# ScalarE splits three weight units of the first expert instead of four ahead of the routing, and loads its function table between the second and the third

## The reference, cut to what matters

```
h = h + rglru_mixer(h, ...)                   # ends with an output projection
logits = rms_norm(h, g) @ router_w            # 256 x 8
top_vals, top_idx = lax.top_k(logits, 2)
top_w = softmax(top_vals)
gates = sum(one_hot(top_idx) * top_w)
for e in range(8):
    y = y + gates[:, e] * ((silu(x @ w_gate[e]) * (x @ w_up[e])) @ w_down[e])
h = h + y
```

## Time and profile before

| what | value |
|---|---|
| median of 3 executions | 1358.57 us (1357.74 to 1360.34) |
| profiled execution, its own time | 1354.03 us |
| profiled execution, its span | 1352.2 us |
| TensorE busy | 1316.0 us (97%) |
| VectorE busy | 799.3 us (59%) |
| ScalarE busy | 639.1 us (47%) |
| mean granted TensorE clock | 0.991 |

### The profile page before, as it was taken

How to read it: one execution, slowest core, us unless ns; L and a number is a source line. 1 busy time by engine, 2 the same in 40 slices (tenths; PEclk the granted TensorE clock), 3 DMA queues, 4 the chain that set the end, 5 groups by cost and what they waited for, 6 DMA issues and landing times.

```text
span 1352.2 us, 18615 instructions
## 1 busy us (share of the span) xinstructions
PE 1316.0 (97%) x7440; PEld 995.3 (74%) x7440; DVE 799.3 (59%) x832; ACT 639.1 (47%) x591; POOL 0.4 (0%) x6
## 2 busy tenths in 40 slices
PE   8999999999999899999999999999999999999997
PEld 7988999999999788884357885346887345888432
DVE  7995565655599679971039981009983105987100
ACT  5486534443488567741048760008872005875000
POOL 0000000000000000000000000000000000000000
PEclk9999999999999979999999999999999999999999
DMA  9332555455365599999999999999999999999996
GB/s 333 128 94 63 156 166 178 138 193 178 111 196 194 223 363 362 363 366 346 406 413 411 409 411 403 401 407 410 414 409 408 412 409 410 412 406 413 409 408 271
DMA packets 149893, 426.13 MB, mean 315 GB/s; under 512 B 7728, under 2 KB 65712, under 8 KB 135472
## 3 DMA queue, kind: packets, MB, share of 16 engines
q1 hardware_dynamic: 149808, 424.90, 82.7%
HBM read 423.82 MB, written 1.05 MB: 314 GB/s over the span
## 4 chain that ended last, share of the span: by engine, by line
PE 77%; DMA 8%; DVE 7%; ACT 3%; issue 3%; SPq 2%; DVEq 0%; ACTq 0%
PE P L1688 55%; PE P L2125 12%; DMA over_gates_raw<-in_moe_w_gate 6%; PE P L2149 3%; DVE cacc L1115 2%; DVE raw_lo L1075 2%; DMA over_xb_raw<-in_moe_w_down 2%; PE P L2012 1%; SPq L602 1%; PE P L2033 1%; DMA raw<-in_w_in_even 1%; PE P L2067 1%; ACT whi L929 1%; PE P L1721 1%; PE P L2030 1%
## 5 line engine op out<-in xcount | busy, mean ns | idle before, releaser
L1443 DVE TENSOR_TENSOR raw_lo<-raw,whi 128x2048 fp32r<-128x2048 f32 x84 | 189.3, 2288 | 10.8 <-ACT whi L929 10.2
L1688 PE MATMUL P<-hn_hi,whi 128*128 128x272 f32 (+1 forms) x640 | 186.4, 291 | 0.5 <-ACT ig L867 0.2
L929 ACT ACTIVATE whi<-raw 128x2048 fp32r<-128x2048 f32 x84 | 161.1, 1920 | 54.2 <-PE P L1688 32.9
L1688 PE MATMUL P<-whi,xe_hi 128*128 128x512 f32 x448 | 179.1, 400 | 7.1 <-DVE over_gates_lo L1443 7.1
L1688 PE MATMUL P<-hn_hi,raw_lo 128*128 128x272 f32 (+1 forms) x640 | 184.5, 288 | 0.0
L1688 PE MATMUL P<-hn_lo,whi 128*128 128x272 f32 (+1 forms) x640 | 183.8, 287 | 0.0
L1688 PE MATMUL P<-whi,xe_lo 128*128 128x512 f32 x448 | 177.3, 396 | 0.0
L1443 DVE TENSOR_TENSOR over_gates_lo<-over_gates_raw,whi 128x2048 fp32r<-128x2048 f32 x72 | 162.9, 2289 | 19.2 <-ACT whi L929 19.1
L1075 DVE TENSOR_TENSOR raw_lo<-raw,whi 128x2048 fp32r<-128x2048 f32 (+4 forms) x71 | 148.1, 2105 | 41.6 <-ACT whi L662 41.5
L929 ACT ACTIVATE whi<-over_gates_raw 128x2048 fp32r<-128x2048 f32 x72 | 137.6, 1919 | 43.1 <-PE P L1688 17.9
L1663 DVE TENSOR_TENSOR hb<-silu,P 128x512 f32<-128x512 f32 (+1 forms) x16 | 9.9, 621 | 220.2 <-PE P L2125 220.2
(11 more groups left out here) (298 smaller groups left out, 2054.4 us busy)
## 6 DMA issues: line engine op xcount, KB each, us to landing
raw<-in_moe_w_up SPq DMA_DIRECT2D x64, 1024.0 KB, 15.3
raw<-in_moe_w_gate SPq DMA_DIRECT2D x64, 1024.0 KB, 15.1
over_gates_raw<-in_moe_w_down SPq DMA_DIRECT2D x64, 1024.0 KB, 16.3
over_gates_raw<-in_moe_w_gate SPq DMA_DIRECT2D x48, 1024.0 KB, 18.5
raw<-in_moe_w_down SPq DMA_DIRECT2D x40, 1024.0 KB, 15.6
over_gates_raw<-in_moe_w_up SPq DMA_DIRECT2D x32, 1024.0 KB, 16.4
over_xb_raw<-in_moe_w_up SPq DMA_DIRECT2D x16, 1024.0 KB, 15.0
raw<-in_ffn_w_gate SPq DMA_DIRECT2D x10, 1024.0 KB, 5.3
```

Of the source, the lines that this page charges most:

```text
L929: act.activation(whi[u % HI][:, :], moe_raw[k % MOE_RAW][:, :], ACT.Copy).then_inc(hi_ready, 1)
L1443: dve.tensor_tensor(moe_lo(k), moe_raw[k % MOE_RAW][:, :], whi[u % HI][:, :].bitcast(F32), ALU.subtract).then_inc(lo_ready, 1)
L1688: last = pe.matmul(dst, lhs, rhs, start=start and n == 0, stop=stop and n == 2)
```

## The change

ScalarE's list changes, and no other engine's. The split of unit 3 moves from ahead of the routing's steps to behind them, and the load of the table with the square root moves from behind unit 3 to between units 1 and 2.

```diff
-            for k in range(4):
+            for k in range(3):
+                if k == 2:
+                    act.preload_act_table_set("sqrt_and_others")
                 split_item_hi(0, k)
...
-            act.preload_act_table_set("sqrt_and_others")
             def squares(c):
...
             act.activation(st[:, 6:8], st[:, 4:6], ACT.Sqrt).then_inc(h2_root, 1)
-            for k in range(4, READY):
+            for k in range(3, READY):
                 split_item_hi(0, k)
```

## The result

| | before | after |
|---|---|---|
| median of 17 executions each | 1360.16 us (1357.51 to 1363.3) | 1353.26 us (1348.31 to 1357.16) |
| ratio after / before | | 0.9963, 95% interval 0.9951 to 0.9976 |
| span of the profiled execution | 1352.2 us | 1350.0 us |

By the measured ratio the change makes the kernel faster by 0.37%, 5.0 us of 1358.57; the interval reaches from 3.3 to 6.7 us. The two medians lie 6.9 us apart, which is more than that, so only the size of some 5 us is sure and not its tenths. The forecast was 1353.5 us.

What follows compares the result with a forecast made beforehand. The routing was taken to wait for unit 3's transfer through its split in ScalarE's list. Terms 2.78 + 2.3 + 0 = 5.1 us took the median from 1358.57 to 1353.5 us, range 1350.8 to 1356.8.

Steps and rivals of the forecast that it cites:

- What bounds: Ahead of the router's product: routing waits for unit 3's weight transfer, because its split stands ahead in ScalarE's list.
- Table load moved, at no cost: ScalarE, between units 1 and 2: the 1.28 us load delays nothing, with 1.66 us to spare before the residual's half 0.
- First term: Routing up to the router's product: squares and copy come earlier, so the product starts at 470.27 instead of 473.05, 2.78 us.
- Second term: Router's product on TensorE: all 32 matmuls end before the clock falls, 3.6 us instead of 5.91, gaining 2.3 us.
- the idle stretch: TensorE's 2.99 us of idle time ahead of the router's product; with it gone, the clock's fall should not come earlier.
- Third term: Gather on TensorE, 5.82 us before: gain taken as 0, with -0.9 and +2.1 us as bounds.
- Three splits in a row: ScalarE behind the root: three splits take 5.55 us, just use up the 4.26 us idle time and cost nothing.
- Does it last to the end?: Expert 0 to the end: transfers catch up within expert 0, then fixed data at fixed rate, so the end moves 5.1 us.

Runs made afterwards that it cites:

- units only: Kernel before with only unit 3's split moved behind the root, the table load left where it was, now behind unit 2; ratio to before 0.9949.
- three loads: Changed kernel with two more table loads, of other sets, ahead of the one between units 1 and 2; ratio to before 0.9979.
- the filled one: Kernel before with 20 more matmuls, results unused, where TensorE was idle ahead of the router's product; ratio to before 0.9994.
- two ahead: Changed kernel with two units instead of three split ahead of the routing, four in a row behind the root; ratio to before 0.9956.
- before again: Kernel before, unaltered, timed against itself for a second trace; ratio 1.0002.
- before with the attention filled: Kernel before with 8 more matmuls, results unused, in the first layer's attention, where TensorE waits at 96 to 97 us; ratio to before 0.9997.

## Why the prediction was right

*What bounds.* Right. The units only kernel shows that unit 3's split, waiting for its transfer, was what the routing waited for.

*Table load moved, at no cost.* Right: 1.28 us, unit 2's split from 464.67, 1.47 us to spare (1.66 forecast). It also brought nothing, since with three units the load fits behind unit 2 as well. The three loads kernel confirms the price and the point from which it hurts.

*First term, 2.78 us.* Measured 6.49 - 3.70 = 2.79 us.

*Second term, 2.3 us.* In the first pair of traces 5.89 - 3.71 = 2.18 us. On average of the traces it is larger: the three traces of before with nothing added to the routing have 5.89, 6.59 and 6.97 us, the five of the kernels whose product starts at +3.70 and with nothing added there all have 3.71, which makes 6.48 - 3.71 = 2.8 us. What I wrote about its cause was half right. The fall did not come earlier, but it comes without the idle stretch too: the filled one did not stop it, and in three loads it came 5.5 us behind the residual with only 1.01 us of idle time ahead of the product. In 13 traces it came 5.5 to 8.7 us behind the residual. The product that ends at +7.4 is ahead of ten of these falls, the one that starts at +6.5 met the fall in all four of its traces. A fall at +5.5 would catch the changed kernel too. In the seven traces whose product starts at +3.70 or +3.34 it came at +7.7 to +8.7; whether the earlier product keeps early falls away or these seven had luck is not shown.

The timed executions fit the split into two terms. Each has a mean granted clock on record. Among executions with the same clock, those of the changed kernel, units only and two ahead (47 in all) are on average 2.6 us quicker than the 102 of before, near the first term's 2.78 (one execution of before, at 1873 us, is left out). The rest of their advantage, 1.3 of 3.9 us, goes with a higher mean clock, 0.9900 against 0.9887.

*Third term, 0.* The gather took 5.42 us instead of 5.82 in the first pair, 6.73 in the second trace of the changed kernel and 6.75 in the second of before, a little above the 6.7 that I took as the worst. Its length goes up and down with the clock's return, on both sides.

*Three splits in a row.* Right; 0.29 us of idle time was left. That cover is gone with a fourth (two ahead), and it still costs nothing.

*Does it last to the end?* Up to the end of expert 0, wholly. The windows of the changed kernel that answer to the earlier trace rows:

```profile
490.00:492.50 2.50, 2.50 (x12) 2.03 (x11) 2.50 (x2) 1.92 (x1) 0.00 (x0) 1.00 1.02 401
...
600.00:613.70 13.70, 13.70 (x77) 8.92 (x77) 0.69 (x1) 1.64 (x3) 0.00 (x0) 1.00 0.76 260
640.00:700.00 60.00, 56.54 (x307) 25.40 (x304) 9.55 (x9) 10.73 (x11) 0.00 (x0) 1.00 1.03 410
```

The gap at 490 us is filled, and expert 0's output is copied at 608.58 us instead of 613.74, 5.16 us earlier. But the span shrank by 2.2 us only. The stretch from that copy to the end took 738.5 us before and 741.4 after. I had said that behind expert 0 there is a fixed amount of data at a fixed rate; that is the step of the prediction that did not hold. The same sum was right for the median and too large by 2.9 us for this pair of traces, so that 5.0 us came out so near to 5.1 is in part luck; the second timing of the changed kernel gave 0.9982, 2.4 us. From copy to copy of the large experts' outputs and the small ones', the changed kernel's trace loses 1.6 us between 913.75 and 1039.24 (125.5 us, against 123.9 from 919.00 to 1042.94) and 1.9 us behind it until 1132.61 (93.4 against 91.4); what differs elsewhere, +0.7, -0.7 and -0.4 us, comes to about nothing. At the head of the first of these stretches, where the fourth expert after expert 0, a large one, begins, the windows of the changed kernel show the clock (all engines):

```profile
912.00:916.00 4.00, 4.00 (x12) 3.10 (x11) 3.73 (x2) 3.84 (x3) 0.00 (x0) 0.57 1.03 410
```

It was low for 3.4 us from 912.4 on. TensorE loses half of that in an expert in which it is hardly quicker than the transfers. That it then frees slots later than they are wanted at that expert's end is my reading. The windows of 1000 to 1100 us, before, then after:

```profile
1000.00:1100.00 100.00, 97.84 (x454) 54.22 (x454) 29.95 (x25) 23.27 (x20) 0.00 (x0) 1.00 1.02 412
```

```profile
1000.00:1100.00 100.00, 97.84 (x448) 52.35 (x448) 26.45 (x23) 20.49 (x18) 0.00 (x0) 0.98 1.00 394
```

The other traces show the price of such a fall in its own stretch. There are three stretches from a small expert's copy to the next large one's in each of the 13 traces. In 22 of these 39 the clock fell shortly ahead of the small expert's copy (at 701 to 705, 912 to 921, or 1128 to 1139 us), and these 22 last 125.3 to 125.6 us; the other 17 last 123.9 to 124.0. So a fall there costs some 1.5 us at once, wherever it comes. The first of these stretches, in before and in before again, as ScalarE's copies at its ends:

```profile
702.83 0.58 ACT L982 ACTIVATE ys<-P 128x512 f32<-128x512 f32 x1
...
826.79 1.02 ACT L984 ACTIVATE ys<-P 128x1024 f32<-128x1024 f32 x1 [5.04 <-PE P L1688]
```

```profile
705.18 0.58 ACT L982 ACTIVATE ys<-P 128x512 f32<-128x512 f32 x1
...
830.66 1.02 ACT L984 ACTIVATE ys<-P 128x1024 f32<-128x1024 f32 x1 [5.04 <-PE P L1688]
```

That is 123.96 and 125.48 us; before again has the fall, at 702.55 us. From expert 0's copy to the end only one of the three places stands out. The seven traces with a fall at 912 to 921 us have 740.4 to 742.5 us, the six without have 737.6 to 739.8. A fall near 702 us hardly shows there: before with the attention filled has one, and still 737.6 us. Why the one at 912 us does, no run shows.

The fall at 912 us came in seven of the nine traces of kernels with an earlier product and in none of the four others, the one at 702 us in two of the nine and in three of the four. Whether the change makes the costly one more frequent, so that a part of the gain is given back, or these 13 fell so by chance, stays open; no experiment was made for it. The two ratios of the changed kernel, 0.9963 and 0.9982, allow either.

## What to carry to other kernels

An instruction that is early work for later (here a split that waits for its transfer) should not stand ahead of a critical chain in an engine's list if its input may land later than the chain's. Look for the engine's wait that ends last, and put such work behind the chain, where the same engine would be idle; the place had 4.26 us here and took one more unit at 1.85 us, and a second one, free of charge. Moving a start by a few microseconds can be worth more than the move, when a stretch of thin matmuls (few columns each) then ends before the clock falls; look at several traces for how early it can fall. And when one execution differs from the next by 0.4%, count in the trace from a common event, and use the timed ratio only for the sum.

## What the runs showed of the hardware

The clock fell in the first layer's attention, at 97 to 99 us for 10.2 us, in six of ten traces of kernels with the same instructions there, after an idle stretch of about 1 us, and that set all of the program behind it back by about 5 us. It is the largest single difference between traces that I found. The profiled execution of before, 4.5 us quicker than the median, had no such fall; that this is the reason for its distance is likely and not shown. Its mean clock fits: it is 0.991, and the 41 timed executions of before with 0.990 or more average 1354.7 us, the 36 with 0.987 or less 1360.7 us.

Table loads follow each other at 1.29 us with no drain, under full transfers as well.

The router's product, 32 matmuls of 8 columns, kept TensorE busy at 0.50 for up to 6.97 us without the clock coming back. In all 13 traces it came back within the gather, 32 matmuls of 128 columns.

A fall of 3.4 us at the head of a large expert makes the stretch to that expert's copy 1.5 us longer, 125.5 us instead of 123.9, in each of 22 cases.
